# The entry of a two-block transformer kernel: first modulation chunk on ScalarE's DMA queue and ahead of the filter taps, its rows turned by transposes and added by VectorE

## What is computed

```python
def adaln(cond, w_mod, b_mod):
    m = jax.nn.silu(cond) @ w_mod + b_mod
    return _split(m, (D_MODEL, D_MODEL, D_MODEL))     # shift, scale, gate

for layer in range(DEPTH):
    sh_l, sc_l, ga_l = adaln(c, w_mod[layer], b_mod[layer])
    sh_c, sc_c, ga_c = adaln(c_ctx, w_mod[layer], b_mod[layer])
    h_lat = rms_norm(x_lat, g_pre[layer]) * (1 + sc_l[:, None]) + sh_l[:, None]
    h_ctx = rms_norm(x_ctx, g_pre[layer]) * (1 + sc_c) + sh_c
    ...                                               # even layer: hyena filter and attention
```

## Time and profile before

| | us |
|---|---|
| median of 3 runs | 1829.55 (1828.61 to 1833.85) |
| the profiled execution, its own time | 1825.82 |
| its span | 1824.0 |
| TensorE busy | 1768.1 (97%) |
| VectorE, ScalarE, GpSimd busy | 1133.6, 905.4, 47.1 |
| mean DMA | 147 GB/s over the span, 268 MB |

### The profile page before, as it was taken

One profiled execution on the slowest core, in us unless ns is written; L12 is line 12 of the kernel. 1 busy time (PEld: TensorE's weight loads), 2 busy tenths in 40 slices (PEclk: granted clock), 3 DMA queues, 4 the chain that ended last, 5 costly groups with the idle time before them and its releaser, 6 DMA issues. The chain is left out here.

```text
span 1824.0 us, 23944 instructions
## 1 busy us (share of the span) xinstructions
PE 1768.1 (97%) x9160; PEld 1454.9 (80%) x9160; DVE 1133.6 (62%) x2031; ACT 905.4 (50%) x1428; POOL 47.1 (3%) x67
## 2 busy tenths in 40 slices
PE   9999999999998999999999999999999999999998
PEld 4867788777886777778778788799887888779986
DVE  6563466688338446766766674766546666576644
ACT  4332444433336256665656456465435646546533
POOL 0000000000000010000100010000000002000000
PEclk9999999999999999999999999999999999999999
DMA  9556221222335344443544444555555344455562
GB/s 341 192 174 208 93 70 47 70 70 70 138 104 185 92 127 125 145 127 119 185 143 137 139 150 160 168 181 185 185 191 170 122 150 139 163 166 181 184 209 80
DMA packets 116169, 268.33 MB, mean 147 GB/s; under 512 B 5388, under 2 KB 9773, under 8 KB 115864
## 3 DMA queue, kind: packets, MB, share of 16 engines
q1 hardware_dynamic: 111528, 252.52, 42.2%
q0 software_dynamic: 3696, 11.98, 2.1%
q10 hardware_dynamic: 832, 2.30, 0.4%
HBM read 265.66 MB, written 1.13 MB: 146 GB/s over the span
## 5 line engine op out<-in xcount | busy, mean ns | idle before, releaser
L144 DVE TENSOR_TENSOR qw_rest<-weights,qw_lead 128x1024 fp32r<-128x1024 f32 (+2 forms) x428 | 519.8, 1217 | 438.9 <-ACT qw_lead L307 437.4
L307 ACT ACTIVATE qw_lead<-weights 128x1024 fp32r<-128x1024 f32 (+2 forms) x428 | 448.2, 1049 | 503.2 <-PE psum L153 490.8
L153 PE MATMUL psum<-qw_lead,b_h_lead 128*128 128x512 f32 (+1 forms) x480 | 197.0, 410 | 1.7 <-ACT b_mqk L2903 0.9
L153 PE MATMUL psum<-qw_lead,b_h_rest 128*128 128x512 f32 (+1 forms) x480 | 186.6, 389 | 0.0
L153 PE MATMUL psum<-qw_rest,b_h_lead 128*128 128x512 f32 (+1 forms) x480 | 186.0, 388 | 0.0
L153 PE MATMUL psum<-b_h_lead,qw_lead 128*128 128x256 f32 x512 | 145.3, 284 | 2.0 <-DVE b_h_rest L641 2.0
L153 PE MATMUL psum<-b_h_lead,qw_rest 128*128 128x256 f32 x512 | 144.9, 283 | 0.0
L153 PE MATMUL psum<-b_h_rest,qw_lead 128*128 128x256 f32 x512 | 144.9, 283 | 0.0
L153 PE MATMUL psum<-e_h_lead,qw_lead 128*128 128x512 f32 x320 | 141.0, 441 | 1.8 <-DVE e_qT L1420 1.4
L153 PE MATMUL psum<-e_h_lead,qw_rest 128*128 128x512 f32 x320 | 125.8, 393 | 0.0
L153 PE MATMUL psum<-e_h_rest,qw_lead 128*128 128x512 f32 x320 | 125.0, 391 | 0.0
(11 more groups left out here) (487 smaller groups left out, 3418.0 us busy)
## 6 DMA issues: line engine op xcount, KB each, us to landing
weights<-in_w_in SPq DMA_DIRECT2D x48, 1024.0 KB, 5.1
weights<-in_o_w_in SPq DMA_DIRECT2D x32, 1024.0 KB, 5.3
weights<-in_w_mlp_up SPq DMA_DIRECT2D x32, 1024.0 KB, 5.3
weights<-in_w_mlp_down SPq DMA_DIRECT2D x32, 1024.0 KB, 4.9
weights<-in_e_w_in SPq DMA_DIRECT2D x26, 1024.0 KB, 5.1
weights<-in_w_mod SPq DMA_DIRECT2D x24, 1024.0 KB, 7.4
weights<-in_e_w_out SPq DMA_DIRECT2D x8, 1024.0 KB, 4.9
weights<-in_o_w_out SPq DMA_DIRECT2D x8, 1024.0 KB, 4.9
```

The lines of the kernel that those rows point to most:

```text
L144: return eng.tensor_tensor(self.rest[at], src, self.lead[at].bitcast(F32), ALU.subtract)
L153: mm = nc.tensor.matmul(out, l, r, start=start and i == 0, stop=stop and i == 2)
L307: self.core.nc.scalar.activation(self.buf.lead[self.at(u)], self.raw(u), ACT.Copy).then_inc(self.lead_ready, 1)
```

## The change

`Enter.load` leaves h = 0 and 1 to `Enter.begin`, which issues them on ScalarE's queue behind `cols` and `ident`. The ten multiplications of the identity at -23.2 go. The planned times of mods0 move: sums 0 and 1 to -23.3 and -23.25, ahead of the taps, the others and the turns a little earlier too. `by_dve` is dropped, so ScalarE copies chunk 0. `turns` for j < 4 transposes the four 128-column blocks of the copied bank into a whole PSUM bank; VectorE then adds the four partials of each with one reduction (128 x 8 x 4) into `columns` in SBUF and raises `summed`, for which the next turn waits instead of for `mod_ready`; `takes` reads `columns`. This holds for mods1 as well.

```diff
@@ Mods.__init__
-        self.rows_out, self.spread, self.taken, self.mod_ready = s("rows_out"), s("spread"), s("taken"), s("mod_ready")
+        self.rows_out, self.spread, self.taken, self.mod_ready, self.summed = s("rows_out"), s("spread"), s("taken"), s("mod_ready"), s("summed")
+        self.columns = core.small[:, 216:248]
@@ Mods.turns
-                done = sum(2 for z in self.chunks[:i] if z[1] in (2, 3))
+                done = sum(1 for z in self.chunks[:i] if z[1] < 4)
                 if done:
-                    pe.wait_ge(self.mod_ready, done)
+                    pe.wait_ge(self.summed, done)
                 for b in range(4):
-                    o = (4 * j + b) * 2
-                    mm = nc.tensor.matmul(ps[:, self.spread_bank[0], o:o + 2], self.rows[i % len(self.rows)][:, b * P:(b + 1) * P], sel, start=True, stop=True)
+                    mm = nc.tensor.transpose(ps[:, self.spread_bank[0], b * P:(b + 1) * P], self.rows[i % len(self.rows)][:, b * P:(b + 1) * P], self.core.ident[:])
@@ Mods.takes
-            elif j >= 2:
-                yield self.turn_at[i] + self.lags[2] - self.lags[1]
-                dve.wait_ge(self.spread, i + 1)
-                m = ps[:, self.spread_bank[0], 0:32].rearrange("p (h k s) -> p h k s", h=2, s=2)
+                continue
+            yield self.turn_at[i] + self.lags[2] - self.lags[1]
+            dve.wait_ge(self.spread, i + 1)
+            parts = ps[:, self.spread_bank[0], :].rearrange("p (b c r) -> p b r c", b=4, c=4)[:, :, 0:2, :]
+            nc.vector.tensor_reduce(self.columns[:, 8 * j:8 * j + 8].rearrange("p (b s) -> p b s", s=2), parts, AX.X, ALU.add).then_inc(self.summed, 1)
+            if j >= 2:
+                dve.wait_ge(self.summed, sum(1 for z in self.chunks[:i + 1] if z[1] < 4))
+                m = self.columns.rearrange("p (h k s) -> p h k s", h=2, s=2)
@@ Enter.__init__
-        self.idle = [(-24.5, 7), (-23.2, 10)]
+        self.idle = [(-24.5, 7)]
@@ Enter.load
-        for h in range(Stream.RAW):
+        for h in range(2, Stream.RAW):
             core.stream.load(sp, h)
@@ Enter.begin
         act.dma_start(core.ident[:], a["ident"]).then_inc(self.consts, 16)
+        for h in range(2):
+            core.stream.load(act, h)
         act.wait_ge(self.consts, 32)
@@ even_layer
-    mods0 = Mods(core, "m0_", r, [(0, 0), (0, 2), (0, 1), (0, 3)], range(u, u + 8), [-20.6, -18.1, -15.6, -15.0, -10.5, -9.9, -7.0, -6.4],
-                 (r.qs[:, 4608:5120],), (4,), (5,), lambda pe: enter.wait_rows(pe), lambda pe: None, lags=(0.65, 2.0, 2.3), by_dve=(0,), turn_at=(-14.3, -12.7, -7.3, -4.4))
+    mods0 = Mods(core, "m0_", r, [(0, 0), (0, 2), (0, 1), (0, 3)], range(u, u + 8), [-23.3, -23.25, -18.2, -18.1, -13.2, -13.1, -8.8, -8.7],
+                 (r.qs[:, 4608:5120],), (4,), (5,), lambda pe: enter.wait_rows(pe), lambda pe: None, lags=(0.65, 2.0, 2.3), turn_at=(-20.8, -15.5, -10.3, -7.3))
```

## The result

The changed kernel takes 1832.88 us (median of 20 runs, 1829.29 to 1837.04), the kernel before 1827.92 us (20 runs, 1825.89 to 1833.85). The medians differ by 5.0 us; the ratio estimated from all runs is 1.0022, 95% interval 1.0014 to 1.0031, which is 4.0 us slower, 2.6 to 5.7. The time is inside the predicted range and the difference is under 0.3%, but the kernel is slower and the interval leaves out no change, where the forecast had +0.1 us. The profiled execution took 1833.9 us, span 1832.1, against 1825.82 and 1824.0 before.

What follows compares the result with a forecast made beforehand. TensorE, busy 97% of the span, was taken as the bound. Terms -5.2 + 2.0 + 2.3 + 0.3 + 0.7 = +0.1 us, put on the median 1829.55, gave 1829.7 (chance 0.48), range 1825.5 to 1834.0.

Steps and rivals of the forecast that it cites:

- Sums and turns, -5.2: TensorE's entry and layer 1: sums 0 and 1 ahead of the taps gain 2.0 us, turns by transposes 3.2.
- The loads, +2.0, bounds 0 and +3.0: Before the taps: w_mod's halves ahead of decay make it land at 15.9, so the taps start 2.0 us later.
- the gap before 5 us: Low DMA share for about 0.9 us in the first 5 us, which the halves can fill; 1.0 us given back.
- The clock, +2.3, bounds -0.2 and +4.5: TensorE in the taps: clock rises only at 21.0, half of 5.1 us lost, less 0.24: +2.3 us.
- The hole before spectrum 0, +0.3: TensorE waits for VectorE's fourth product; turn 0 covers only half of what sum 0 covered: +0.3 us.
- The hole at the x turns, +0.7: X turns 2 and 3 wait for ScalarE's leads, with only turn 2 between instead of sums 4 and 5: +0.7 us.
- At nothing: VectorE's reductions (0.2 us), ScalarE's extra copy and issues, SyncE's x and x's scaling delay nothing: no cost.
- A: Rival at the loads: the halves cost decay nothing, taps start at 13.9; -2.8 us, 1826.8; chance 0.28.
- C: Rival at the loads: ScalarE's queue is served behind SyncE's, halves come no earlier; +2.2 us, 1831.8; chance 0.04.
- B: Rival at the taps: decay 3.0 us late and clock up only 9.4 us after they start; +3.0, 1832.6; chance 0.15.
- decay at 15.9: Sign before the taps: decay lands near 15.9 instead of 11.5 and the taps start there.
- a stretch of about 36.6 us: Sign on TensorE: first tap to first dense product takes longer than 33.3 us by about 3.3.

Runs made afterwards that it cites:

- e2_queue: Kernel before with only the first two halves of w_mod moved to ScalarE's queue; sums, turns and ten pads as before: 1836.05 us, ratio 1.0042.
- a0_again: The changed kernel run and profiled once more, unchanged: 1832.77 us, ratio 1.0022 to the kernel before.
- e4_small: Changed kernel, but ScalarE issues the two halves of w_mod only after the filter's small inputs have landed: 1832.67 us, ratio 1.0026 to the kernel before.
- e3_pads: Changed kernel with pads added, 7 identity multiplications between sums 0 and 1 and 14 behind sum 1: 1830.13 us, ratio 1.0010 to the kernel before.
- q_one: Kernel before with only the first half of w_mod (load 0) on ScalarE's queue: 1826.37 us, one run only.
- b0_again: The kernel before run and profiled once more, unchanged: 1827.19 us, one run.
- e1_turns: Kernel before with only the turns by transposes and VectorE's reductions, the first reduction ahead of the scaling of x: 1825.92 against 1828.12 us, ratio 0.9985.
- b2_copy: e1_turns with VectorE instead of ScalarE copying chunk 1 and its reduction placed early: 1828.67 against 1828.9 us, ratio 0.9999 to the kernel before.
- b1_again: Repeat of b2_copy's edits plus sum 4 and spectrum 4 ahead of the x turns; this kernel's two sets: ratios 1.0001 and 0.9990 to the kernel before.
- n1_nopads: Kernel before without its ten pads, nothing else changed: 1829.26 against 1826.63 us, ratio 1.0013.

## Why the time came out in the range, and which terms were wrong

*Sums and turns, -5.2.* Right. The two sums left the stretch at 0.99 us each. Turns measured 0.44 to 0.50 in the entry (forecast 0.48), a gain of 1.6; in layer 1 0.35 to 0.44 (forecast 0.41), a gain of 1.8 for four. -5.4 in all.

*The loads, +2.0, bounds 0 and +3.0.* This is the term that was mis-sized: +3.8, outside the bounds, in this profile, and +4.4 and +4.5 in e2_queue and a0_again. Two steps of it failed. The 1.0 us that the gap before 5 us was to give back didn't come: from 3 to 5 us the changed kernel moved 235 GB/s, the one before 225, 20 KB more in all. The DMA rates of the kernel before and then of the changed one behind that:

```profile
5.00:8.00 3.00, 3.00 (x15) 3.00 (x14) 2.22 (x6) 0.42 (x1) 0.00 (x0) 1.00 1.11 211
8.00:12.00 4.00, 4.00 (x16) 3.02 (x16) 2.38 (x9) 0.15 (x1) 0.00 (x0) 1.00 1.03 392
```

```profile
5.00:8.00 3.00, 1.76 (x5) 1.04 (x6) 0.61 (x2) 0.00 (x0) 0.00 (x0) 1.00 1.11 352
8.00:12.00 4.00, 3.99 (x23) 2.57 (x21) 2.52 (x8) 0.42 (x1) 0.00 (x0) 1.00 1.02 255
```

From 5 to 12 us the changed kernel moved 3 x 352 + 4 x 255 = 2076 KB, the kernel before 3 x 211 + 4 x 392 = 2201 KB: no more bytes, only in another order, the small ones now later. So the full 5.4 us are paid. And I had counted what the 2 MB do to decay, but not what they do to the small inputs ahead of it: those land at 6.24 instead of 3.97, SyncE's issues take longer (2.10 us for one of 0.63), decay is issued 1.7 us late. e4_small shows that undoing this brings decay's landing from 17.6 to 16.9. Of decay's delay of 6.1 us the taps saw 3.8, because they had 2.4 us of slack; the prediction counted that slack rightly for the one execution that it had. It was not typical: in the six other profiles whose first loads go as before, the taps began at 11.57 to 13.03 and not at 13.87.

*The clock, +2.3, bounds -0.2 and +4.5.* That the taps would run slow was right, the way there and the size were not: +4.4 in the account, 4.2 by e3_pads, just inside the bounds. I had the clock still low when the sums ran and rising 5.1 us into the taps. In fact it was up by 10.35, behind the first seven pads (layer 2's pair takes 0.57 us from 10.35 to 10.92, 1.05 before), sum 0 ran fast, and the two waits took the clock away again, to come back 9.5 us into the taps. What failed is that I priced the waits as late work and not as a cause of a fall. The second half of w_mod, estimated to land at about 12.2, let sum 1 go only at 13.58. With decay later than forecast the wait was longer too: the two errors go the same way, which independent bounds don't show.

*The hole before spectrum 0, +0.3.* Nothing: at the slow clock the turn covers VectorE's product. *The hole at the x turns, +0.7.* +0.6, in two waits of 0.30 and 0.26 ahead of x turns whose order was forecast.

*At nothing.* The reductions are 0.18 to 0.19 us and nobody waited for one in the changed kernel. One statement was wrong: that x is scaled in time. ScalarE's copy of chunk 1 now stands ahead of the squares of x and waited 4.41 us for its sums, so the squares start at 32.70 instead of 24.90 and the scaling ends at 42.12, where the x turns begin at 42.18. ScalarE's and VectorE's timelines of after:

```profile
32.21 0.60 ACT L999 ACTIVATE e_qT<-psum 128x512 f32<-128x512 f32 x1 [4.41 <-PE psum L988]
39.38 2.74 DVE L1150 TENSOR_SCALAR x_res<-x_res,small 128x1024 f32<-128x1024 f32 x4
```

Here it costs 0.2 us, since all else is late too. In e3_pads, where TensorE is quicker, the same x turns begin at 39.43.

*The rivals.* A (decay is not delayed) is refuted by decay's landing in after, e2_queue, q_one and e4_small. C (ScalarE's queue is served behind SyncE's) is refuted by sum 0 at 10.92 on data that came by that queue ahead of decay. B, delay and low clock together, is what happened: it gave +3.0, the ratio says +4.0 (2.6 to 5.7). Its deciding point, delay and clock over 4.2 us together, was passed with 3.8 + 4.4. It fell short in the delay, whose worst case I had set too low. The absolute time was off by 3.2 us, less than the difference was (3.9 by the ratio, 4.9 by the medians), because the three runs of the table before had a median 1.6 us above that of the twenty.

So there is luck in the range. The sum that I gave 0.48 didn't come; rival B, given 0.15, did. 1832.88 lies below 1834.0 because B and the spread of single runs had opened the range that far. Of the signs named ahead, the length of the turns came, and no hole after the taps was over 1 us; decay at 15.9, the rise of the clock near 21, the first dense product near 52.6 and a stretch of about 36.6 us did not (17.6, 27, 56.44 and 38.74).

## What to carry to other kernels

When a load is moved ahead of others, add its bytes to the landing of every transfer behind it that someone waits for, small ones and their issues too, and don't count on gaps in the DMA row unless the bytes moved show them. When a new wait opens on TensorE, price it together with the clock: here waits of 1.6 and 3.05 us cost another 4.2 us in the work behind them, and pads put into those waits brought that back in the trace. Split a change of several edits into its parts: here the turns alone gain 2.7 us, and the loads alone lose 7.7. And profile the kernel before more than once: its first profile had the taps 1.7 us later than its second, and whether the clock falls behind one and the same wait differs between executions.

## What the runs showed of the hardware

- *The clock's rise and its falls differ between executions.* The same 20 pad records, after the same work, took 4.63 us in the earlier trace rows and 2.50 in b0_again, begun 0.15 us apart. Behind waits of 1.3 to 3 us in the entry it fell in many runs (b0_again 1.33, e1_turns 2.72, b2_copy 2.25), and stayed up behind q_one's 1.18, and in b1_again behind one of 1.46. Behind the same wait of 2.28 us near 933 it fell in 7 of 14 profiles.
- *The column of the granted clock can be silent.* In n1_nopads it reads 1.00 over the taps, while their duration, 7.19 us against 3.7, tells 1.2 GHz; likewise in the kernel before, up to 14 us (the prediction read the level from the spacing of records). In both no change of the clock had been recorded yet. In the traces here I trust the column only after its first change. The row of n1_nopads:

```profile
15.00:20.00 5.00, 5.00 (x10) 1.42 (x12) 2.37 (x4) 0.00 (x0) 0.00 (x0) 1.00 1.05 387
```

- *One 1 MB transfer on another queue seems enough to delay small ones.* The first matmul, which waits for small transfers issued from 0.74 to 2.2 us, started at 5.8 to 6.7 us in all five profiles with a large load on ScalarE's queue from 1.65 (6.04 in q_one, the only profile with one), and at 3.7 to 4.0 in eight of the nine others. It was 5.19 in b2_copy, whose loads go as before, and I have no reason for that. The Trainium skill (DMA: Bandwidth & Descriptors, section Queues, rings and completion order) says that a completion is written only after all earlier writes of that DMA engine, across its queues. That would delay a small transfer by what others have under way; no run here tells it from plain sharing of the engines.
- *Four transposes of 128 x 128 in float32 take about half as long as four matmuls with two columns*: 0.35 to 0.50 us at the high clock against 0.81 to 0.92.
